# A hybrid decoder trunk on one core: the last expert job's down units in plain float32, its order, and its gathers

## The reference

```python
logits = xf @ router
top_v, top_i = lax.top_k(logits, 2)            # of 8 experts
gates = jax.nn.softmax(top_v, axis=-1)
# tokens grouped by expert, each group through its expert:
yb = (silu(xb @ w_gate[e]) * (xb @ w_up[e])) @ w_down[e]   # 1024 -> 1344 -> 1024
y  = zeros.at[buf_tok].add(yb * buf_gate)
h  = h + y
out = rms_norm(h, final_norm)
```

## Time and profile before

| | us |
|---|---|
| runs (3): median, lowest, highest | 1061.5, 1060.24, 1061.85 |
| the profiled execution: its own time | 1059.15 |
| its span, first to last instruction | 1057.3 |
| TensorE (PE) busy in the span | 1012.5 |
| VectorE (DVE) busy | 600.9 |
| ScalarE (ACT) busy | 453.7 |
| GpSimd (POOL) busy | 72.6 |

### The profile page before, as it was taken

One profiled execution on the slowest core, in us unless ns is written; L12 is line 12 of the kernel. 1 busy time (PEld: TensorE's weight loads), 2 busy tenths in 40 slices (PEclk: granted clock), 3 DMA queues, 4 the chain that ended last, 5 costly groups with the idle time before them and its releaser, 6 DMA issues.

```text
span 1057.3 us, 15079 instructions
## 1 busy us (share of the span) xinstructions
PE 1012.5 (96%) x5506; PEld 870.5 (82%) x5506; DVE 600.9 (57%) x816; ACT 453.7 (43%) x603; POOL 72.6 (7%) x138
## 2 busy tenths in 40 slices
PE   5999999999999999999999799999999999999974
PEld 4887887788888888888888699999887888888763
DVE  6585676254444434343438650110788989898877
ACT  6535554243242222222125300101687777777734
POOL 2200000000000101000000030000000000000240
PEclk9999999999999999999999989999999999999996
DMA  9021311525462737364426657795999999999992
GB/s 285 2 80 40 123 67 66 164 101 158 135 185 90 210 99 217 101 197 132 126 79 217 241 208 233 257 344 167 364 364 389 370 391 367 375 392 359 392 378 105
DMA packets 150155, 226.55 MB, mean 214 GB/s; under 512 B 16676, under 2 KB 97572, under 8 KB 150112
## 3 DMA queue, kind: packets, MB, share of 16 engines
q1 hardware_dynamic: 138464, 187.98, 52.8%
q0 software_dynamic: 10832, 37.44, 10.1%
q10 hardware_dynamic: 816, 0.54, 0.2%
HBM read 196.92 MB, written 29.02 MB: 214 GB/s over the span
## 4 chain that ended last, share of the span: by engine, by line
PE 87%; DVE 7%; DMA 3%; ACT 2%; issue 1%; SPq 0%; POOLq 0%; DVEq 0%; ACTq 0%
PE bank L1191 22%; PE bank L1193 22%; PE bank L1192 22%; PE bank L1595 7%; PE bank L1619 4%; DMA u_raw<-in_moe_w_down 2%; PE bank L1363 1%; DVE w_lo L1772 1%; PE bank L1574 1%; PE bank L1203 1%; PE bank L1343 1%; PE bank L1354 1%; PE bank L1500 1%; DVE scratch L1784 1%; PE bank L1699 1%
## 5 line engine op out<-in xcount | busy, mean ns | idle before, releaser
L2251 DVE TENSOR_TENSOR u_lo<-u_raw,u_hi 128x2048 fp32r<-128x2048 f32 (+1 forms) x108 | 217.5, 2046 | 12.6 <-ACT u_hi L1063 12.5
L1063 ACT CAST u_hi<-u_raw 128x2048 fp32r<-128x2048 f32 (+1 forms) x108 | 185.1, 1723 | 72.8 <-DMA u_raw<-in_moe_w_up 39.3
L1191 PE MATMUL bank<-big_hi,w_lo 128*128 128x512 f32 (+2 forms) x352 | 134.4, 382 | 0.0
L1193 PE MATMUL bank<-big_hi,w_hi 128*128 128x512 f32 (+2 forms) x352 | 134.3, 381 | 0.0
L1192 PE MATMUL bank<-big_lo,w_hi 128*128 128x512 f32 (+2 forms) x352 | 134.2, 381 | 0.0
L1772 DVE TENSOR_TENSOR w_lo<-stage_own,w_hi 128x1024 fp32r<-128x1024 f32 (+1 forms) x89 | 103.3, 1206 | 13.6 <-ACT w_hi L818 13.6
L1191 PE MATMUL bank<-u_hi,nx_lo 128*128 128x512 f32 (+1 forms) x288 | 106.5, 370 | 0.0
L1005 ACT ACTIVATE scratch<-bank 128x512 f32<-128x512 f32 x21 | 12.6, 598 | 218.8 <-PE bank L1193 218.8
L1193 PE MATMUL bank<-u_hi,nx_hi 128*128 128x512 f32 (+1 forms) x288 | 104.5, 363 | 0.0
L1192 PE MATMUL bank<-u_lo,nx_hi 128*128 128x512 f32 (+1 forms) x288 | 104.4, 363 | 0.0
L2029 DVE TENSOR_TENSOR scratch<-scratch,bank 128x512 f32<-128x512 f32 x21 | 14.4, 688 | 151.7 <-ACT scratch L1005 151.7
(11 more groups left out here) (342 smaller groups left out, 1691.6 us busy)
## 6 DMA issues: line engine op xcount, KB each, us to landing
u_raw<-in_moe_w_gate SPq DMA_DIRECT2D x68, 512.0 KB, 7.6
u_raw<-in_moe_w_up SPq DMA_DIRECT2D x68, 512.0 KB, 8.5
u_raw<-in_moe_w_down SPq DMA_DIRECT2D x64, 512.0 KB, 7.4
stage_own<-in_ffn_w_gate SPq DMA_DIRECT2D x21, 512.0 KB, 6.2
stage_own<-in_ffn_w_up SPq DMA_DIRECT2D x21, 512.0 KB, 7.5
stage_own<-in_ffn_w_down SPq DMA_DIRECT2D x21, 512.0 KB, 4.4
xbuf<-scratch POOLq DMA_DIRECT2D x21, 496.0 KB, 6.2
u_raw<-in_moe_w_down SPq DMA_DIRECT2D x8, 1024.0 KB, 8.4
```

The lines of the kernel that those rows point to most:

```text
L1063: s.copy(u_hi[u % HIS][0:rows, 0:size], u_raw[u % RAWS][0:rows, 0:size]).then_inc(n_hi, 1)
L1191: t_.matmul(dst, st_lo, mv_hi, start=start, stop=False, skip_group_check=check)
L1193: return t_.matmul(dst, st_hi, mv_hi, start=False, stop=stop, skip_group_check=check)
L2251: v.tensor_tensor(u_lo[u % RAWS][0:rows, 0:size], u_raw[u % RAWS][0:rows, 0:size], u_hi[u % HIS][0:rows, 0:size], ALU.subtract).then_inc(n ...
```

## The change

Four things, all in or just ahead of the last narrow job:

1. Units 16 and 17 aren't split any more. TensorE multiplies the raw unit by the unsplit activations (`na_full`, written by the new `act_out(2)`) in plain float32, one matmul in place of three.
2. New orders. ScalarE: hi 11, silu(1), hi 12, 13, act_hi_out(1), hi 14, silu(2), hi 15, table load, act_out(2). VectorE: product(1), lo 12, 13, add_y(0), act_lo_out(1), lo 14, add_y(1), product(2), lo 15, add_slots, add_y(2), then norms 0 and 1, add_y(3), norms 2 and 3.
3. POOL: the slots' gather from `hbuf` is issued ahead of the loop over narrow jobs; after the loop come `y_rows` 0 and 1, then a wait until block 0's pair has landed, the two other slot gathers, a wait until block 1's pair has landed, `y_rows(2)`, the wait for add_y(0), and `y_rows(3)`.
4. The slots' first half (bank 4) is added when its own last matmul is done (`slot_half`).

```diff
+LAST_SPLIT = 2
+        na_full = [over(f"na_full{n}", [P, 4, P], "act_hi_mem", 1024 + 512 * n, F32) for n in range(2)]
 # POOL
+            def slot_rows(n):
+                dst, src = ((slot_h, hbuf), (slot_a, ybuf), (slot_b, ybuf))[n]
+                pool.indirect_dma_start(out=dst, out_offset=None, in_=src, ...
+                                        ).then_inc(slot_landed, 16)
+            pool.wait_ge(slots_known, 1)
+            pool.wait_ge(h_stored, 16 * T)
+            slot_rows(0)
             narrow = pool.value_load(...)
             with pool.Fori(0, narrow) as n:
...
-            pool.wait_ge(slots_known, 1)
-            pool.wait_ge(h_stored, 16 * T)
-            for t in range(T - 1):
-                y_rows(t)
-            for n, (dst, src) in enumerate(((slot_h, hbuf), (slot_a, ybuf), (slot_b, ybuf))):
-                pool.indirect_dma_start(...).then_inc(slot_landed, 16)
+            for t in range(2):
+                y_rows(t)
+            pool.wait_ge(y_gathered[0], 32)
+            slot_rows(1)
+            slot_rows(2)
+            pool.wait_ge(y_gathered[1], 32)
+            y_rows(2)
             pool.wait_ge(h_final, 1)
             y_rows(T - 1)
 # ScalarE
+                def act_out(f):
+                    act.wait_ge(n_turned, n * 3 + (f + 1))
...
+                        s.copy(na_full[0][:, 0:2, :], bank[6][:, 0:2 * P]...)
+                        s.copy(na_full[0][0:FTAIL, 2, :], bank[6][0:FTAIL, 2 * P:3 * P]).then_inc(n_act_hi, 1)
                 act_hi_out(0)
-                for u in (11, 12):
-                    unit_hi(u, n)
+                unit_hi(11, n)
+                if final:
+                    silu(1)
+                    unit_hi(12, n)
+                    unit_hi(13, n)
+                    act_hi_out(1)
+                    unit_hi(14, n)
+                    silu(2)
+                    unit_hi(15, n)
+                    s.activation(warm[:, 0:1], eps_t[:, 0:1], ACT.Sqrt)
+                    act_out(2)
+                    return
+                unit_hi(12, n)
                 silu(1)
 # TensorE
                 def down_pair(f, j):
                     u = DN_AT[f] + j
-                    pe.wait_ge(n_lo, n * NU + (u + 1))
+                    plain = final and f >= LAST_SPLIT
+                    if plain:
+                        pe.wait_ge(n_landed[u % RAWS], n_landings(u, n))
+                    else:
+                        pe.wait_ge(n_lo, n * NU + (u + 1))
...
+                            if plain:
+                                last = t_.matmul(bank[4 + half][:, :], na_full[f % 2][0:rows, 2 * j + c, :],
+                                                 u_raw[u % RAWS][0:rows, at], start=False, stop=tail)
+                            else:
+                                last = mm3(...)
+                            if final and tail and half == 0:
+                                last.then_inc(slot_half, 1)
...
-                pe.wait_ge(n_act_lo, n * 3 + 3)
+                pe.wait_ge(n_act_hi if final else n_act_lo, n * 3 + 3)
 # VectorE
                 if final:
-                    for t in range(T):
-                        unit_lo(12 + t, n)
-                        if t == 2:
-                            act_lo_out(1)
-                        add_y(t)
-                    unit_lo(16, n)
-                    unit_lo(17, n)
-                    product(2)
-                    add_slots()
-                    act_lo_out(2)
+                    unit_lo(12, n)
+                    unit_lo(13, n)
+                    add_y(0)
+                    act_lo_out(1)
+                    unit_lo(14, n)
+                    add_y(1)
+                    product(2)
+                    unit_lo(15, n)
+                    add_slots()
+                    add_y(2)
                     return
...
-            for t in range(T):
-                final_norm(t)
-            dve.wait_ge(n_used, narrow * NU + (RAWS + NU))
+            final_norm(0)
+            final_norm(1)
+            add_y(3)
+            final_norm(2)
+            final_norm(3)
             for half in range(2):
+                if half == 0:
+                    dve.wait_ge(slot_half, 1)
+                else:
+                    dve.wait_ge(n_used, narrow * NU + (RAWS + NU))
                 v.scalar_tensor_tensor(slot_y[:, at], bank[4 + half][:, :], ...)
```

More of the change, by code:

```diff
@@ L451, in trunk @@
         slot_landed = sem("slot_landed")
+        slot_half = sem("slot_half")
         slot_sum = sem("slot_sum")
@@ L1132, in act_hi_out @@
                         s.copy(na_hi[0][0:FTAIL, 2, :], bank[6][0:FTAIL, 2 * P:3 * P]).then_inc(n_act_hi, 1)
+                def act_out(f):
+                    act.wait_ge(n_turned, n * 3 + (f + 1))
+                    if f < 2:
+                        s.copy(na_full[f][:, :, :], bank[6][:, :].rearrange("p (c n) -> p c n", c=4)).then_inc(n_act_hi, 1)
+                    else:
+                        s.copy(na_full[0][:, 0:2, :], bank[6][:, 0:2 * P].rearrange("p (c n) -> p c n", c=2))
+                        s.copy(na_full[0][0:FTAIL, 2, :], bank[6][0:FTAIL, 2 * P:3 * P]).then_inc(n_act_hi, 1)
                 for u in (5, 6, 7, 8):
@@ L1147, in narrow_job @@
                     unit_hi(u, n)
[L1148 to L1152, removed]
                 unit_hi(18, n)
@@ L1693, in turn @@
                     pe.wait_ge(n_prod, n * 3 + (f + 2))
-                    if f:
+                    if final and f > LAST_SPLIT:
+                        pe.wait_ge(n_act_hi, n * 3 + f)
+                    elif f:
                         pe.wait_ge(n_act_lo, n * 3 + f)
@@ L1713, in down_pair @@
                             at = slice(c * D + 512 * half, c * D + 512 * half + 512)
-                            last = mm3(bank[4 + half][:, :], hi, lo, u_hi[u % HIS][0:rows, at], u_lo[u % RAWS][0:rows, at],
-                                       f == 0 and j == 0 and c == 0, tail)
+                            if plain:
+                                last = t_.matmul(bank[4 + half][:, :], na_full[f % 2][0:rows, 2 * j + c, :],
+                                                 u_raw[u % RAWS][0:rows, at], start=False, stop=tail)
+                            else:
+                                last = mm3(bank[4 + half][:, :], hi, lo, u_hi[u % HIS][0:rows, at], u_lo[u % RAWS][0:rows, at],
+                                           f == 0 and j == 0 and c == 0, tail)
+                            if final and tail and half == 0:
+                                last.then_inc(slot_half, 1)
                     last.then_inc(n_used, 1)
@@ L1743, in narrow_job @@
                     gate_and_up(2, j)
-                pe.wait_ge(n_act_lo, n * 3 + 2)
+                pe.wait_ge(n_act_hi if final and LAST_SPLIT <= 1 else n_act_lo, n * 3 + 2)
                 down_pair(1, 0)
```

6 lines of the change are left out of this document (3 added, 3 removed).

## The result

The kernel before: median 1061.49 us (4 runs, 1060.24 to 1061.85). The changed kernel: median 1053.84 us (4 runs, 1052.71 to 1055.23), ratio 0.9933 with a 95% interval of 0.9921 to 0.9946. A second set gave 1053.74 against 1061.69, ratio 0.9927 (0.9914 to 0.994). The forecast was 1055.1, its range 1053.0 to 1058.6. The profiled execution took 1052.94 with a span of 1051.1, where the table of the kernel before has 1059.15 and 1057.3. The four runs of the changed kernel form two pairs, 1052.71 and 1052.94 at a mean granted clock of 0.992 and 1054.73 and 1055.23 at 0.990; the profiled execution belongs to the first pair, and the median lies between them.

The account below looks back on a forecast made before the run. VectorE's queue in the last job sets the end, starting late by a landing that one copy needn't wait for. The profiled 1059.15 minus 6.4 is 1052.75; with the 2.35 offset, 1055.1 us, range 1053.0 to 1058.6.

Parts of the forecast that it names:

- the three signs of being wrong: VectorE waits for a gather; TensorE's last matmul releases the slot's adds; the first narrow job shows a new TensorE gap.
- The sum for the profiled execution: Whole kernel: the profiled 1059.15 us minus 6.4 us from the last job gives 1052.75.
- case B: Last job: unit 14 lands earlier, so lo 14 follows act_lo_out(1) directly; slot's adds 7.1 us earlier.
- the rival of earlier landings: Last job: unit 13 lands earlier too and all behind moves with it, 2 us more, 1052.4; chance 0.09.
- "Cost nothing" for the waits between the gathers: POOL in the last job: despite the waits, gathers land by when they are wanted; cost nothing, 0.1 us at the bound.
- The middle between cases A and B: Last job's gain taken midway between landings as before (5.8 us) and unit 14 landing earlier (7.1 us): 6.4 us.
- The offset to the median: The median of the runs lies 2.35 us above the profiled execution, assumed the same after the change.
- Cover was looked for at unit 10 only: First narrow job: 4 us of slack at unit 10 hides the slot rows 0 gather; cost nothing, without cover 1.3 us.
- The plain matmul's price: TensorE, units 16 and 17: 0.43 us per plain matmul of 512 columns, 2.6 us for six.
- The rival of TensorE as the end: Last job: twice the plain price at the lower clock makes TensorE last, 1.7 us lost, 1056.8; chance 0.07.

Follow-up runs that it names:

- Orders only: The changed kernel with units 16 and 17 split again, new orders, gathers and waits kept: 1057.73 us, ratio 0.9966 to the kernel before.
- plain only: The kernel before with units 16 and 17 in plain float32 and nothing else, old orders and gathers: 1058.61 us, ratio 0.9969.
- copy first: The kernel before with only act_hi_out(1) moved ahead of unit 14 on ScalarE in the last job: 1060.92 us, ratio 0.9986.
- Slot rows 0 last: The changed kernel with the slots' hbuf gather issued after y_rows(3) and add_slots moved behind add_y(3): 1053.42 us.
- the kernel with both late: The changed kernel with units 14 and 15 plain, row block 2 gathered before slot rows 1 and 2, slot rows 0 gathered last, add_slots behind add_y(3): 1051.41 us.
- the doubled matmuls: The changed kernel with each plain matmul of units 16 and 17 issued twice: 1053.32 us.

## Why the prediction was right, and where it was not

*The place and the mechanism.* TensorE's wait was the copy's place behind two landings, VectorE's list set the end (in the earlier trace rows TensorE was last by another 0.66), and the change took both: first wait 0.24 and ended by lo 14, no VectorE gap above 0.3, adds 6.19 earlier (5.8 to 7.1 expected), TensorE done 5 us ahead of them. "Orders only" and "plain only" show that both halves count, 4.0 and 3.1 us each by itself. No gather came late either: row block 3's two gathers issued in 0.95 and 2.46 us, inside the spread of the earlier trace rows, and nothing waited for them. One of the three signs of being wrong came, though: the new TensorE gap in the first narrow job.

*Two terms were wrong and cancelled.* The sum for the profiled execution was 1052.75; it took 1052.94. That it fits so closely is luck. The sum had 6.4 for the last job and nothing for the first narrow one. The last job gained 8.21: case B's 7.1, and unit 13's cast 1.46 earlier from the mark (14.23 to 12.77), as in the rival of earlier landings, less the 0.27 that lo 14 still waits, makes 8.3. Against it stand 1.5 from the first narrow job, which the prediction had at nothing, and 0.5 that no instruction of the change explains.

*"Cost nothing" for the waits between the gathers.* The step asked only whether a wait would make a gather late. None was late, so that much was right. But it left out most of what the waits give: they keep gathers out of the queues while units 13 and 14 load. Without them, and in the order of before, the kernel takes 3.7 us more. The middle between cases A and B was the only place where this could enter, with 0.64.

*The offset to the median.* I carried over 2.35 us from the execution to the median of runs; after the change it is 0.90 (1053.84 less 1052.94). These 1.45 less are more than the whole 1.26 us by which the forecast was high. The experiment with the copy first shows what may lie behind it: in the kernel before, unit 13's landing moves by 5 us between executions, and the profiled one had it early. None of the 47 other runs of that kernel in these comparisons was as fast as it (the lowest took 1059.36). In other executions the stall that the chain of waits shows need not be the one that counts: in the profiles of "copy first" and "plain only" VectorE waits longest at product(1), 3.69 and 5.24. That the slower runs had such landings is argued from three profiles, not shown run by run. After the change, the two runs at a mean clock of 0.990 may have lost 1.6 of their 2 us to the lower clock of the last section: some 3.5 us at half clock take 0.0017 off the mean clock of 1052 us, an estimate from those rows. No profile shows these two.

*The gather of slot rows 0.* Cover was looked for at unit 10 only; units 16 and 17 and product(2) of the same job had none. Their loads land late behind it, as the wait of 1.67 at 787.07 shows. Issued once, the gather opens gaps of 1.2 to 2.0 in all (five profiles at the upper clock near 752), issued twice of 3.4. That the medians of the kernels with it elsewhere are no better stays partly open. One part is shown: the gap is smaller when TensorE comes to the job late. In the changed kernel's second profile it reached the job about 1.6 us later, counted from the load near 629, and the gap was 0.81:

```profile
752.39 3.49 PE L1691 MATMUL bank<-ident,scratch 128*72 128x128 f32 x16 [0.44 <-ACT scratch L1109]
...
798.67 0.49 PE L1217 MATMUL bank<-u_hi,na_lo 128*128 128x512 f32 x1 [0.81 <-DVE na_lo L2370]
```

With units 14 and 15 plain too, also 1.6 late, there was none. As I read it, a delayed TensorE gives the loads that time. Slot rows 0 last was late by as much, so its profile could win little from a job without the gather. Against the gather as the only cause: the kernel with both late has no early gather, and still a gap of 0.48 there, so that stretch has next to no slack for anything.

*The plain matmul's price.* Sized at 0.43 us from rows of one record, it is 0.89, two records; the earlier trace rows count 16 records of 512 columns, but the attention's eight heads issue one such matmul each, eight in all, and I had not held the one against the other. A pass of the split kind starts every 0.227, so a plain matmul costs 3.9 of them. The Trainium skill ("FP8 and Floating Point Precision", section TensorE Precision Notes) has four passes for true FP32, and the trace agrees with it and not with me. The rival of TensorE as the end needed the low clock too, and the granted clock from 1024 to 1038 was 1.00: with hardly a wait left, it did not fall as in the earlier trace rows. So the price was hidden, as the doubled matmuls show.

## What to carry to other kernels

A wait in front of a transfer is not only a delay of that transfer: when the queues are full, it is a place given to another load, and here the kernel without two such waits lost nearly half of the gain. Read how much a landing moves between executions before a stall in one profile is taken for the limit: moving the one copy that the chain named won 0.9 us, not 3. And an early transfer is free only if every load of the stretch has slack: here the first load had 4 us, and the last ones had none.

## What the runs showed of the hardware that was not expected

The 16 short matmuls that turn the last wide job's product (L1691) take 1.92 us in the changed kernel's first profile (the row below) and 3.49 in its second (the row at 752.39 above), with the same wait of 0.44 before them. In both, TensorE is busy without a gap at a clock of 1.00 for the 16 us ahead of that wait, so nothing in these rows says why the clock falls in one and not in the other. The granted clock tells the two apart, first profile, then second (columns: length, busy time and count of PE, PEld, DVE, ACT and POOL, clock, DMA share, GB/s):

```profile
752.93 1.92 PE L1691 MATMUL bank<-ident,scratch 128*72 128x128 f32 x16 [0.44 <-ACT scratch L1109]
```

```profile
752.00:756.00 4.00, 3.56 (x27) 3.28 (x27) 3.42 (x4) 3.70 (x7) 0.00 (x0) 1.00 1.04 394
```

```profile
752.00:756.00 4.00, 3.61 (x17) 3.16 (x18) 1.84 (x2) 2.12 (x3) 0.00 (x0) 0.57 1.04 404
```

1.00 is the upper level of 2.4 GHz; 0.57 is the mean of a stretch that lies mostly at the lower, 1.2 GHz. Four of the fourteen profiles have it there, far from the change, and each started the narrow jobs about 1.6 us later for it (counted from the load near 629), 0.15% of the kernel's time.
